# Half of the weight sums of a block product moved from VectorE to adding transfers on GpSimd's queue

## What is computed

```python
def pool_mixer(xn, w_in, w_group, scale, w_out):
    ...
    return (mixed * scale * jax.nn.silu(g)) @ w_out      # [256, 4096] @ [4096, 2048]
...
D_FF = ((8 * D_MODEL // 3 + 127) // 128) * 128           # 5504: [256, 5504] @ [5504, 2048], "down"
```

## Time and profile before

| | |
|---|---|
| median of 3 runs | 2436.83 us (2435.7 to 2437.18) |
| span of the profiled execution | 2434.2 us |
| its TensorE, busy | 2423.9 us |
| its VectorE / ScalarE / GpSimd, busy | 1720.3 / 1373.7 / 64.7 us |
| mean granted TensorE clock | 0.999 |
| pooling output, from its first matmul to the end of its last | 457.7 to 628.0 us |
| down, up to the end of the span | 2197.8 to 2434.2 us |

### The profile page before, as it was taken

The page is one execution under the profiler, slowest core; times in us unless marked ns, Lnnn a source line. Parts: engine busy times, 40 slices in busy tenths (PEclk is TensorE's granted clock), DMA queues, the critical chain, the costliest instruction groups (busy, mean ns, idle before and its releaser), DMA issues.

```text
span 2434.2 us, 33996 instructions
## 1 busy us (share of the span) xinstructions
PE 2423.9 (100%) x12679; PEld 2084.6 (86%) x12679; DVE 1720.3 (71%) x2083; ACT 1373.7 (56%) x1823; POOL 64.7 (3%) x79
## 2 busy tenths in 40 slices
PE   9999999999999999999999999999999999999998
PEld 8888888888889999888888888888988888888887
DVE  7675757899765656796756667665767657679887
ACT  6444444556656666565755556565644545455555
POOL 0000000001100000010000000000000000000001
PEclk9999999999999999999999999999999999999999
DMA  8666666565555554565585554454565565656654
GB/s 314 199 189 185 188 189 183 188 218 199 180 175 181 179 158 147 211 212 189 165 235 163 161 171 151 164 178 154 172 191 180 189 190 180 191 169 205 220 184 145
DMA packets 234595, 453.03 MB, mean 186 GB/s; under 512 B 14929, under 2 KB 60417, under 8 KB 233324
## 3 DMA queue, kind: packets, MB, share of 16 engines
q1 hardware_dynamic: 230960, 435.94, 55.9%
q0 software_dynamic: 3120, 14.90, 1.7%
q10 hardware_dynamic: 396, 0.59, 0.2%
HBM read 448.68 MB, written 2.69 MB: 185 GB/s over the span
## 4 chain that ended last, share of the span: by engine, by line
PE 99%; DVE 1%; ACT 0%; issue 0%; ACTq 0%; DVEq 0%
PE ps L813 25%; PE ps L815 13%; PE ps L779 12%; PE ps L781 12%; PE ps L780 12%; PE ps L963 6%; PE ps L964 6%; PE ps L965 6%; PE ps L737 1%; PE ps L844 1%; PE ps L846 1%; PE ps L845 1%; PE ps L1443 1%; PE ps L1214 0%; PE ps L1202 0%; PE ps L1401 0%
## 5 line engine op out<-in xcount | busy, mean ns | idle before, releaser
L2443 DVE TENSOR_TENSOR w_lo<-raw,w_hi 128x1024 fp32r<-128x1024 f32 x689 | 842.1, 1228 | 466.7 <-ACT w_hi L1613 446.8
L1613 ACT ACTIVATE w_hi<-raw 128x1024 fp32r<-128x1024 f32 x689 | 726.8, 1060 | 650.9 <-PE ps L815 357.7
L813 PE MATMUL ps<-x_hi_lo,w_hi 128*128 128x512 f32 x2336 | 821.0, 394 | 0.0
L815 PE MATMUL ps<-x_hi_lo,w_lo 128*128 128x256 f32 x2336 | 660.7, 283 | 0.0
L813 PEld LDWEIGHTS ps<-x_hi_lo,w_hi 128*128 128x128 f32 x2336 | 438.8, 188 | 101.2
L779 PE MATMUL ps<-w_hi,x_hi_lo 128*128 128x512 f32 (+3 forms) x1184 | 461.9, 390 | 0.0
L781 PE MATMUL ps<-w_hi,x_hi_lo 128*128 128x512 f32 (+3 forms) x1184 | 453.7, 383 | 0.0
L780 PE MATMUL ps<-w_lo,x_hi_lo 128*128 128x512 f32 (+3 forms) x1184 | 452.7, 382 | 0.0
L815 PEld LDWEIGHTS ps<-x_hi_lo,w_lo 128*128 128x128 f32 x2336 | 439.3, 188 | 0.0
L1790 ACT ACTIVATE w_hi<-raw 128x1024 fp32r<-128x1024 f32 (+1 forms) x201 | 209.4, 1051 | 169.8 <-PE ps L965 152.2
L2451 DVE TENSOR_TENSOR w_lo<-raw,w_hi 128x1024 fp32r<-128x1024 f32 (+1 forms) x201 | 243.2, 1228 | 35.4 <-ACT w_hi L1790 35.1
(11 more groups left out here) (469 smaller groups left out, 2711.9 us busy)
## 6 DMA issues: line engine op xcount, KB each, us to landing
raw<-in_w_up SPq DMA_DIRECT2D x160, 512.0 KB, 3.9
raw<-in_pool_w_in SPq DMA_DIRECT2D x126, 512.0 KB, 3.8
raw<-in_w_in SPq DMA_DIRECT2D x96, 480.0 KB, 3.8
raw<-in_w_down SPq DMA_DIRECT2D x84, 512.0 KB, 5.1
raw<-in_pool_w_out SPq DMA_DIRECT2D x64, 512.0 KB, 4.8
raw<-in_ple_w_gate SPq DMA_DIRECT2D x64, 512.0 KB, 4.3
raw<-in_mla_w_in SPq DMA_DIRECT2D x56, 448.0 KB, 3.5
raw<-in_pool_w_group SPq DMA_DIRECT2D x32, 512.0 KB, 4.1
```

The lines of the kernel that those rows point to most:

```text
L813: pe.matmul(bank, w_hi[:, slot, cols], xs[:, k].rearrange("p s n -> p (s n)"), start=k == 0, stop=False, skip_group_check=True)
L815: last = pe.matmul(bank[:, 0:T], w_lo[:, slot, cols], xs[:, k, 0, :], start=False, stop=k == nkt - 1, skip_group_check=True)
L1613: act.activation(w_hi[:, t.slot(), :], raw[:, slot, :], ACT.Copy).then_inc(S("w_hi"), 1)
L2443: dve.tensor_tensor(w_lo[:, t.slot(), :], raw[:, u % RAW, :], w_hi[:, t.slot(), :].bitcast(F32), ALU.subtract)\
```

## The change

In pooling output and down, the first two of a quad's sums, T1 = B11 + B12 and T3 = B12 + B22, are no longer VectorE instructions. GpSimd issues a transfer from SBUF to SBUF that adds its source to its destination (`accum_op`), 512 KB each, 28 in all. The first of a quad waits until b11 and b12 have landed and B11's `w_lo` is written; the second waits for the first's completion and for b22. ScalarE waits for both by the semaphore `w_summed`. T2 and T4 stay on VectorE. To make all sums additions, signs of the activations' sums and of the banks' combination are changed (same number of instructions). The seven products no longer stand in one run: `woven` puts the three raw products first and plain steps between the others: B11, B22, B21, plain, plain, T1, T3, plain, T2, (plain in down), T4. The attention layer's output (`MLA_OUT`) keeps its sums on VectorE and its order. Two small loads now share one semaphore. `quads_mixed` and `quads_out` of pair 0 stand after all of its steps. The table of releases follows: b11's slot is free after T2, b12's after T3, b22's and b21's after T4.

```diff
+RAW_BLOCKS, SUM_BLOCKS = ("B11", "B12", "B22", "B21"), ("T1", "T3", "T2", "T4")
+
+
+def woven(n, k, plains):
+
+    q = {part: [(part, n, k)] for part in RAW_BLOCKS + SUM_BLOCKS}
+    return (q["B11"] + q["B22"] + q["B21"] + plains[:2] + q["T1"] + q["T3"] + plains[2:3] + q["T2"] + plains[3:] + q["T4"])
+
+
+def in_one_run(n, k):
+
+    return [(part, n, k) for part in ("B11", "B22", "T1", "T3", "B21", "T2", "T4")]
...
-PQ = [[("quad", n, k)] for n, k in enumerate(POOL_QUADS)]
-POOL_OUT = [P0[:9] + P1[:1] + PQ[0] + P1[1:4] + PQ[1] + P1[4:7] + PQ[2] + P1[7:] + P0[9:],
-            P2[:4] + PQ[0] + P2[4:7] + PQ[1] + P2[7:9] + P3[:1] + PQ[2] + P2[9:] + P3[1:]]
+POOL_OUT = [P0[:8] + P1[:1] + woven(0, 20, P1[1:4]) + woven(1, 24, P1[4:7]) + woven(2, 28, P1[7:]) + P0[8:],
+            P2[:4] + woven(0, 20, P2[4:7]) + woven(1, 24, P2[7:9] + P3[:1]) + woven(2, 28, P3[1:4]) + P2[9:] + P3[4:]]
...
+DOWN = [D0[:10] + woven(0, 24, D1[:4]) + woven(1, 28, D1[4:8]) + woven(2, 32, D1[8:12]) + woven(3, 36, D1[12:] + D0[10:11]) + D0[11:],
+        D2[:4] + woven(0, 24, D2[4:8]) + woven(1, 28, D2[8:12]) + woven(2, 32, D3[:4]) + woven(3, 36, D2[12:] + D3[4:5]) + D3[5:]]
+DOWN_Y_STEPS = {6: 3, 7: 4, 12: 5, 15: 6, 22: 7, 30: 8}
...
+MLA_OUT = [[], M2[:3] + in_one_run(0, 8) + M3[:2] + in_one_run(1, 12) + M2[3:] + M3[2:]]
...
+                if kind == "B11":
+                    begun[c] = len(quads)
+                    quads.append({"unit": first_unit + len(loads)})
+                    j1, j2 = (kts, kts + 1), (kts + 2, kts + 3)
+                    loads += [(j1, 2 * p), (j1, 2 * p + 1), (j2, 2 * p + 1), (j2, 2 * p)]
+                    released += [None] * 4
+                q = quads[begun[c]]
+                q[kind] = products
+                steps[-1].append((kind, c, kts, q["unit"]))
+                if kind == "T4":
+                    for n, part in enumerate(last_product):
+                        released[q["unit"] - first_unit + n] = q[part]
+                last_quad = products + 1
+            products += 1
...
+BY_DMA, BY_VECTOR = ("T2", "T3", "T4", "T4"), ("T3", "T3", "T2", "T4")
...
+            if x.weight_sums and kind in ("T1", "T3"):
+                t.add("w_summed")
+                act.wait_ge(S("w_summed"), 16 * t.n["w_summed"])
+            else:
+                t.add("w_sums")
+                act.wait_ge(S("w_sums"), t.n["w_sums"])
+            product_hi(raw[:, (u + n) % RAW, :])
...
+            product_lo(raw[:, (u + (RAW_BLOCKS if kind in RAW_BLOCKS else SUM_BLOCKS).index(kind)) % RAW, :])
             b11, b12, b22, b21 = (raw[:, (u + n) % RAW, :] for n in range(4))
-            product_lo(b11)
-            dve.wait_ge(S(f"raw_full{(u + 1) % RAW}"), 16 * ((u + 1) // RAW + 1))
-            dve.tensor_tensor(b11, b12, b11, ALU.subtract).then_inc(S("w_sums"), 1)
-            product_lo(b22)
-            dve.tensor_tensor(b12, b22, b12, ALU.subtract).then_inc(S("w_sums"), 1)
-            product_lo(b11)
-            dve.tensor_tensor(b22, b22, b11, ALU.subtract).then_inc(S("w_sums"), 1)
-            product_lo(b12)
-            product_lo(b21)
-            dve.wait_ge(S("w_sums"), t.n.get("w_sums", 0) + 3)
-            dve.tensor_tensor(b21, b21, b22, ALU.subtract).then_inc(S("w_sums"), 1)
-            product_lo(b22)
-            product_lo(b21)
-            t.add("unit", 4)
-            t.add("more", -4)
-            t.add("w_sums", 4)
+            if x.weight_sums:
+                if kind == "T3":
+                    dve.tensor_tensor(b22, b22, b11, ALU.add).then_inc(S("w_sums"), 1)
+                    t.add("w_sums")
+                elif kind == "T2":
+                    dve.wait_ge(S("w_sums"), t.n["w_sums"])
+                    dve.tensor_tensor(b21, b21, b22, ALU.add).then_inc(S("w_sums"), 1)
+                    t.add("w_sums")
+                return
+            if kind == "B11":
+                dve.wait_ge(S(f"raw_full{(u + 1) % RAW}"), 16 * ((u + 1) // RAW + 1))
+                dve.tensor_tensor(b11, b11, b12, ALU.add).then_inc(S("w_sums"), 1)
+            elif kind == "B22":
+                dve.tensor_tensor(b12, b12, b22, ALU.add).then_inc(S("w_sums"), 1)
+            elif kind == "T1":
+                dve.tensor_tensor(b22, b22, b11, ALU.add).then_inc(S("w_sums"), 1)
+            elif kind == "B21":
+                dve.wait_ge(S("w_sums"), t.n["w_sums"])
+                dve.tensor_tensor(b21, b21, b22, ALU.add).then_inc(S("w_sums"), 1)
+            if kind in ("B11", "B22", "T1", "B21"):
+                t.add("w_sums")
...
-            if n in (21, 22):
-                quads_mixed(0, n - 21)
-        for n in (2, 3):
+            if n in (11, 13):
+                y_lo(n // 2 + 1)
+        for n in range(4):
             quads_mixed(0, n)
-        for n, (kind, _, kts) in enumerate(POOL_OUT[1]):
-            step_lo(kind, kts)
+        for n, at_step in enumerate(pool_out.steps[1]):
...
-            if 28 <= n <= 28 + 3:
-                quads_out(0, n - 28)
-        for n, (kind, _, kts) in enumerate(DOWN[1]):
-            step_lo(kind, kts)
+        for n in range(4):
+            quads_out(0, n)
+        for n, at_step in enumerate(down.steps[1]):
+            step_lo(down, *at_step)
...
+        def weight_sums(x):
+
+            for q in x.weight_sums:
+                b11, b12, b22 = (raw[:, (q["unit"] + n) % RAW, :] for n in range(3))
+
+                def arrived(n):
+                    u = q["unit"] + n
+                    pool.wait_ge(S(f"raw_full{u % RAW}"), 16 * (u // RAW + 1))
+
+                def add_to(dst, src):
+                    if t.n["w_summed"]:
+                        pool.wait_ge(S("w_summed"), 16 * t.n["w_summed"])
+                    pool.dma_start(dst, src, accum_op=ALU.add).then_inc(S("w_summed"), 16)
+                    t.add("w_summed")
+
+                arrived(0)
+                arrived(1)
+                pool.wait_ge(S("w_lo"), RAW + q["B11"] + 1)
+                add_to(b11, b12)
+                arrived(2)
+                add_to(b12, b22)
...
             load(pgain, a["post_norm"][n:n + 1, :].broadcast_to([128, D]), "post_gain_in")
+            if n == 0:
+                weight_sums(pool_out)
             pool.wait_ge(S("post_gain_in"), 16 * (n + 1))
...
         load(fgain, a["norm_final_2"].unsqueeze(0).broadcast_to([128, D]), "final_gain_in")
+        weight_sums(down)
         pool.wait_ge(S("final_gain_in"), 16)
```

More of the change, by code:

```diff
@@ L91, with paired_tables @@
 M2, M3 = ([("plain", c, (k, k + 1)) for k in range(0, 8, 2)] for c in (2, 3))
[L92 to L98, removed]
+MLA_OUT = [[], M2[:3] + in_one_run(0, 8) + M3[:2] + in_one_run(1, 12) + M2[3:] + M3[2:]]
+def paired_tables(first_unit, pairs, before, last_product):
+    loads, released, quads_end, plain_end, steps, quads = [], [], [], {}, [], []
@@ L99, in quad_tables @@
     last_quad = 0
     products = first_unit + before
-    for p, steps in enumerate(pairs):
-        for kind, c, kts in steps:
+    for p, pair in enumerate(pairs):
+        begun = {}
+        steps.append([])
+        for kind, c, kts in pair:
             if kind == "plain":
+                steps[-1].append((kind, c, kts, first_unit + len(loads)))
                 loads.append((kts, c))
                 released.append(products)
-                products += 1
-                plain_end[c] = products
-            else:
[L109 to L113, removed]
+                plain_end[c] = products + 1
+            else:
+                if kind == "B11":
[12 more added lines that the diff above has]
+            products += 1
@@ L451, in build, with __init__ @@
     class Paired:
-        def __init__(self, name, y, yh, yl, tiles, sums, sums_hi, sums_lo, quads, steps, loads, quads_end, plain_end, pairs_before):
+        def __init__(self, name, y, yh, yl, tiles, sums, sums_hi, sums_lo, quads, steps, loads, quads_end, plain_end, pairs_before, weight_sums):
             self.name, self.y, self.yh, self.yl, self.tiles = name, y, yh, yl, tiles
@@ L1008, in block, with part @@
                         cols = slice(n * 512, n * 512 + 512)
-                        last = times(dst, yh_[:, n], yl_[:, n], wh[:, cols], wl[:, cols], n == 0 and begins(name), final and n == 1)
+                        last = times(dst, yh_[:, n], yl_[:, n], wh[:, cols], wl[:, cols], n == 0 and begins(bank), closing[bank] == i and n == 1)
                     last.then_inc(S("w_used"), 1)
                     t.add("more")
-                def quad(q, k):
+                def part(i, name, q, k):
@@ L1015, in quad @@
                     e1, e5, e6, e7 = x.quad_banks(p)
-                    c, last = 2 * p, q == len(x.quads) - 1
-                    y_ready(k)
+                    c = 2 * p
                     y1, y2 = slice(k, k + 2), slice(k + 2, k + 4)
                     t0, t1 = slice(0, 128), slice(128, 256)
[L1020 to L1023, removed]
-                    else:
```

(16 more changed lines are left out.)

192 lines of the change are left out of this document (98 added, 94 removed).

## The result

The changed kernel took 2519.85 us (median of 4 runs, 2518.3 to 2521.66) against 2436.6 us (4 runs, 2435.7 to 2437.18): ratio 1.0343, 95% interval 1.0329 to 1.0358. It is 83 us slower. The direction was forecast and the time lies inside the range; the forecast of 33 us more is too small by 50.

What follows compares the result with a forecast made beforehand. TensorE was taken as the bound. Stalls of 13.0 us in pooling output and 14.4 in down, 1.5 between pairs and 4 for the queue sum to 33 us, giving 2470 us; own range 2442 to 2520, widened to 2440 to 2550.

Steps and rivals of the forecast that it cites:

- VectorE's relief: Both stages: the 28 VectorE sums that go, 34 us, lie beside TensorE and give back nothing.
- matmul pitch: Rival, both stages: VectorE's instructions hold up the pitch; shortening by 1.2% would give 2432 us; chance 0.04.
- queue term of 4 us for `post_gain`: Pooling output's first quad: the first add stands behind post_gain's 1 MB load on GpSimd's queue, costing 4 us.
- the cost of raw products and releases: Both stages: no term; only a failure clause said adding transfers might delay SP's loads until raw products stall.
- 1.1 us for sharing the engines: Each adding transfer: 1.1 us of its price for sharing the engines with four loads then under way.
- X: Price of one adding transfer, from when it may be issued to its landing: 5.8 us, a quad's two 11.6.
- slope of 20 us for each us of X: Whole kernel: the summed loss moves by about 20 us for each us of X above 5.8.
- such a wait: Both stages, after a pair's last late T3: the plain step and T4 wait for VectorE, 1.4 us a pair.
- Hidden adds: Rival: with X at most 4.2 us the adds fit in all gaps but pooling output's; 2439 us, chance 0.15.
- The Trainium skill's fit: Transfer on GpSimd's path: 2.0 us plus bytes over 436 GB/s, 3.2 us an add; time about 2437 us.
- Slow adds: Rival: adding costs engines more than a second read, X passes 8.3; 83 us at 8.3, chance 0.17.
- The clause on SP's loads in the last part: Both stages: prediction fails if adding transfers delay SP's loads so much that the raw products stall too; no size.

Runs made afterwards that it cites:

- e8: Changed kernel without transfers: all four sums on VectorE in woven order, T2 summed behind T1 and T4 behind T3, slots back earlier; 2439.8 us.
- e12: Against e8, T2 summed in b11's slot, slots given back at T2, T3, T3 and T4, no transfers; 2457.93 us.
- e1: Changed kernel with all four sums on VectorE and no transfers, its order and table of releases kept; 2463.72 us.
- e6: Changed kernel with post_gain's load issued behind the twelve adds of pooling output, not ahead of the first; 2516.74 us.
- e4: Changed kernel with whole adds, but SP's loads of both stages bring only 64 of each 512 columns; 2465.59 us.
- e2: Changed kernel with its transfers copying in place of adding, so T1 and T3 multiply b12 and b22; 2487.95 us.

## Why the prediction was right and wrong

The medians in one line of steps:

| kernel | us | step |
|---|---|---|
| before | 2436.3 | |
| e8: woven order | 2439.8 | +3.5 |
| e12: b11 (and b12) back two products later | 2457.9 | +18.1 |
| e1: b22 back one or two products later, T2 and T4 summed later | 2463.7 | +5.8 |
| after: the 28 adds | 2519.9 | +56.2 |

**Right.** VectorE's relief gave nothing, and matmul pitch did not gain by it: from 566 to 586 us TensorE started 88 matmuls with VectorE busy for 13.4 of the 20 us, as in the earlier trace rows. T3 is where the chain of two adds holds ScalarE, VectorE and TensorE. The queue term of 4 us for `post_gain` measured 3.1 (e6), as far as that can be told. The add alone was priced well: fixed 1.5 plus two passes of 1.6 is 4.7 us, and it took 4.5.

**Failed: the cost of raw products and releases, taken as nothing.** The text asks only "whether the new path of T1 and T3 fits behind TensorE", and of the load of b12 it says that it "lands in 3.4 us, earlier". The slots of b11, b12 and b22 are given back later and SP loads in ring order, so the loads from the next quad's B22 and B21 on start late and in a burst, land in up to 9.5 us in e1's pooling output and 12.2 beside the adds (6.9 before), and B22 and B21 wait for them. e8, e12 and e1 show 24 us for that, T2's and T4's later sums included, and 3.5 for the order: 27 of the 50 us that the forecast lacked.

**Failed: "1.1 us for sharing the engines".** X was 5.8 us for each of the two. The second add needs none of the 1.1, since it finds the engines free. The first meets the burst of five or six loads and takes 8.6 us in the mean. The pair took 13.2 us in the mean, and 0.5 us between landing and next issue, in place of 11.6. The forecast's own slope of 20 us for each us of X makes of (13.7 - 11.6) / 2 = 1.05 us another 21, so 54 us for the adds, where e1 to after measured 56.2. That the two agree so closely is luck, for the places are others. With 13.7 us for the pair the forecast's terms give stalls at T3 of about 46 us; the trace has 23.5, less than even the 26 of the forecast with 11.6. TensorE, already late by its stalls at B22 and B21, comes to T3 later than the forecast counted, which leaves the adds more time; this reason is argued from the order of the gaps and no run tested it. By the starts of the matmuls, e1 to after is about 23.5 us at T3, 5 more at B22 and B21, 15 more at plain products and T4 (behind seven of the eleven stalled T3 the plain product stalls another 0.7 to 0.8 us, where the forecast had such a wait for the last quad of a pair only), and 12 of longer pitch. And in e4, with 10.0 us for the pair and the same 0.5 between, the forecast's sum gives some 23 us and 29 were measured.

**Missing: the clock.** The forecast had no term for it. After the stall at T3 of the third quad TensorE's matmuls (the kernel after) read:

```profile
550.14 0.80 PE L987 MATMUL ps<-w_hi,pool_y_sums_hi 128*128 128x512 f32 x1 [3.37 <-DVE w_lo L2480]
550.73 0.63 PE L988 MATMUL ps<-w_lo,pool_y_sums_hi 128*128 128x512 f32 x1
551.16 0.63 PE L989 MATMUL ps<-w_hi,pool_y_sums_lo 128*128 128x512 f32 x1
```

and the granted clock of two stretches behind that stall (last columns but two):

```profile
550.00:555.00 5.00, 4.86 (x11) 3.81 (x12) 4.71 (x5) 1.32 (x2) 0.00 (x0) 0.50 0.05 3
556.00:560.00 4.00, 4.00 (x19) 3.25 (x18) 3.43 (x4) 2.86 (x3) 0.00 (x0) 1.00 0.94 286
```

0.50 is 1.2 of 2.4 GHz; starts are 0.43 us apart and then 0.23 again. The trace has six such stretches in the two stages, 23.8 us together, two more of them being

```profile
637.50:640.90 3.40, 2.95 (x7) 2.40 (x8) 3.40 (x4) 1.14 (x2) 0.00 (x0) 0.50 0.01 2
2344.20:2347.60 3.40, 3.40 (x8) 2.72 (x9) 2.96 (x3) 1.87 (x3) 0.00 (x0) 0.50 1.05 290
```

They hold 9 of the 15.6 us of longer pitch in the first table. Most of the rest is that the second start behind a gap comes 0.33 us after the first in place of 0.23, at a granted clock of 1.00 too:

```profile
534.47 0.50 PE L987 MATMUL ps<-w_hi,pool_y_sums_hi 128*128 128x512 f32 x1 [1.25 <-DVE w_lo L2480]
...
534.80 0.39 PE L988 MATMUL ps<-w_lo,pool_y_sums_hi 128*128 128x512 f32 x1
```

e1 has no stretch at 0.50, and its 3.6 us of longer pitch are mostly of that second kind. So the clock is 9 of the 56 us of the adds. It comes with the stalls and is not a cost of its own; no run took it away alone.

**The rivals.** Hidden adds fell: the mechanism needed X of at most 4.2, and even alone an add takes 4.5. The Trainium skill's fit in DMA: Bandwidth & Descriptors, Anatomy of one DMA, gives an estimate of 3.2 us; a plain copy alone took 2.8 (e2), near it, but an add 4.5. Slow adds (X over 8.3 for each) was half true: the first add passed 8.3 in most quads, not because adding costs more, but because of what stands beside it. The clause on SP's loads in the last part was the right warning, given no price and no chance.

## What to carry to other kernels

When a sum moves from a compute engine to a transfer, price the buffers that it holds: here a slot of the load ring given back two products later cost 18 us, a third of what the adds themselves did, and the ordered load queue passed it on to every load behind, those with free slots too. A transfer beside a burst waits for the burst's engine time as well as its own: here two in series (13.7 us) did not fit into some 11 us where one (8.3) did. Price the relief of an engine at zero until a wait of the bound engine names it.

## What was not expected of the hardware

An adding transfer of 512 KB within SBUF occupies the sixteen DMA engines for 2.6 to 2.8 us, against 1.6 for a 512 KB load, and lands in 4.5 us alone (copy 2.8, half size 3.2). Of the eleven stalls of TensorE of over 2 us in the kernel after, six came with a stretch at the lower clock level, the five longest (2.9 to 3.5 us) and one of 2.2 us at 2344 us; others of 2.4 and 2.6 us did not (at 523 and 611 us). Such a stretch adds to the stall: at 550 us 3.5 us of gap and 2.6 of longer pitch behind it.
